# Stick-breaking attention by sigmoids and a running product, in a two-layer attention trunk

## Reference

```python
z = einsum('bhqd,bhkd->bhqk', qb, k) * scale
mask = kpos[None, :] < qpos[:, None]
log1m = where(mask, log_sigmoid(-z), 0.0)
between = cumsum(log1m, axis=3, reverse=True) - log1m
a = where(mask, exp(log_sigmoid(z) + between), 0.0)
out = einsum('bhqk,bhkd->bhqd', a, v)
```

## Time and profile before

| | us |
|---|---|
| median of 3 runs | 827.91 (827.84 to 828.54) |
| the profiled execution | 828.2 |
| its span in the profile | 826.4 |
| TensorE busy | 821.6 (99%) |
| VectorE busy | 559.7 (68%) |
| ScalarE busy | 477.8 (58%) |
| GpSimd busy | 293.7 (36%) |

### The profile page before, as it was taken

The page is one execution under the profiler, slowest core; times in us unless marked ns, Lnnn a source line. Parts: engine busy times, 40 slices in busy tenths (PEclk is TensorE's granted clock), DMA queues, the critical chain, the costliest instruction groups (busy, mean ns, idle before and its releaser), DMA issues.

```text
span 826.4 us, 11044 instructions
## 1 busy us (share of the span) xinstructions
PE 821.6 (99%) x4050; PEld 673.7 (82%) x4050; DVE 559.7 (68%) x821; ACT 477.8 (58%) x715; POOL 293.7 (36%) x297
## 2 busy tenths in 40 slices
PE   9999999999999999999999999999999999999998
PEld 5888888888888888888888888888788888888886
DVE  5576889868865666655454688898697666666542
ACT  6886655785465554543457775567844645454441
POOL 0078784404303432320000889653061044323100
PEclk9999999999999999999999999999999999999999
DMA  9745877684558777785565556878745687877652
GB/s 332 271 138 178 222 230 219 182 247 131 203 178 229 199 230 212 223 221 183 167 203 195 162 192 192 224 222 210 223 153 178 206 214 218 230 223 212 215 184 71
DMA packets 119637, 167.76 MB, mean 203 GB/s; under 512 B 56608, under 2 KB 59040, under 8 KB 119328
## 3 DMA queue, kind: packets, MB, share of 16 engines
q1 hardware_dynamic: 119296, 166.79, 66.9%
q10 hardware_dynamic: 288, 0.27, 0.1%
HBM read 153.40 MB, written 1.05 MB: 187 GB/s over the span
## 4 chain that ended last, share of the span: by engine, by line
PE 98%; DMA 1%; issue 0%; SPq 0%; ACT 0%; DVE 0%
PE acc L732 91%; PE att L812 1%; PE att L895 1%; PE att L779 1%; PE att L886 1%; DMA w_raw<-in_w_in 1%; PE att L804 1%; PE acc L812 1%; PE att L853 0%; PE att L869 0%; PE att L908 0%; PE att L972 0%; PE att L963 0%; PE att L854 0%; PE att L839 0%
## 5 line engine op out<-in xcount | busy, mean ns | idle before, releaser
L1234 DVE TENSOR_TENSOR w_lo<-w_raw,w_hi 128x1024 fp32r<-128x1024 f32 (+1 forms) x276 | 365.4, 1337 | 147.1 <-ACT w_hi L996 144.6
L732 PE MATMUL acc<-w_hi,xt 128*128 128x512 f32 (+1 forms) x1728 | 432.3, 392 | 0.5 <-ACT xt L1019 0.3
L996 ACT ACTIVATE w_hi<-w_raw 128x1024 fp32r<-128x1024 f32 (+1 forms) x275 | 286.1, 1051 | 168.7 <-PE acc L732 159.1
L732 PEld LDWEIGHTS acc<-w_hi,xt 128*128 128x128 f32 x1728 | 319.0, 188 | 66.3 <-issue 1.3
L732 PE MATMUL acc<-w_lo,xt 128*128 128x512 f32 (+1 forms) x864 | 229.9, 388 | 0.0
L732 PEld LDWEIGHTS acc<-w_lo,xt 128*128 128x128 f32 x864 | 162.0, 188 | 32.9
L1485 POOL TENSOR_SCALAR small<-small 128x2 f32<-128x2 f32 (+4 forms) x14 | 10.4, 745 | 209.2 <-ACT sq_dump L1096 132.4
L1617 POOL COPY hid_t<-hid_halves_t 128x512 uint16<-128x512 uint16 x44 | 37.7, 885 | 94.3 <-DMA hid_halves_t<-hid_halves 80.0
L1608 POOL COPY hid_halves<-hid 128x512 uint16<-128x512 uint16 x44 | 45.6, 1064 | 65.2 <-DVE hid L1311 65.2
L1625 POOL TENSOR_TENSOR merged<-merged,prod 128x1024 f32<-128x1024 f32 x10 | 32.5, 3250 | 61.2 <-DVE prod L1283 60.3
L732 PE MATMUL acc<-w_hi,ht_hi 128*128 128x512 f32 x176 | 47.7, 390 | 0.0
(11 more groups left out here) (175 smaller groups left out, 723.5 us busy)
## 6 DMA issues: line engine op xcount, KB each, us to landing
w_raw<-in_w_ffn SPq DMA_DIRECT2D x88, 512.0 KB, 4.2
w_raw<-in_w_gate SPq DMA_DIRECT2D x64, 512.0 KB, 3.9
w_raw<-in_w_ffn_down SPq DMA_DIRECT2D x44, 512.0 KB, 4.0
w_raw<-in_w_in SPq DMA_DIRECT2D x39, 512.0 KB, 4.7
w_raw<-in_w_branch SPq DMA_DIRECT2D x16, 512.0 KB, 4.1
w_raw<-in_w_out SPq DMA_DIRECT2D x16, 512.0 KB, 3.3
bg<-in_b_gate SPq DMA_DIRECT2D x8, 512.0 KB, 5.4
w_raw<-in_w_in SPq DMA_DIRECT2D x8, 396.0 KB, 3.4
```

What stands on the lines that cost most here:

```text
L732: return pe.matmul(acc[bank0 + t][:, 0:N], x_part[:, k0 + k, t * P:(t + 1) * P], w_part[:, k, 0:N], start=first, stop=last)
L996: act.activation(w_hi[:, n % WR, :, 0:N], w_raw[:, n % RAW, :, 0:N], copy).then_inc(s_hi, 1)
L1234: dve.tensor_tensor(w_lo[:, n % WR, :, 0:N], w_raw[:, n % RAW, :, 0:N], w_hi[:, n % WR, :, 0:N].bitcast(F32), ALU.subtract).then_inc(s_lo, 1)
```

## The change

Mixer A takes the form of C and D, with queries on the partitions. The scores of both pairs are computed at slot 9, the second in an idle bank of acc; the mask product goes. VectorE adds the strict mask (a constant) while it reads the banks into eb. ScalarE writes sigmoid(-z) of all four heads to a new buffer za (4 x 384 columns) and sigmoid(z) back to eb (step ssig, slot 10). VectorE runs, from the last key backwards, a scan over each head's 384 columns of za, state = max(state * za, restart), where restart is 1 at the two places where a row of queries ends (step sscan, slots 11 and 12), and multiplies eb by za shifted by one column (step smul, slots 12 and 13). GpSimd deals the halves of both pairs at slot 13 (rank 0.2, so before prep B in its queue), SyncE transposes at slots 21 and 22, ScalarE joins them into za at slots 18 and 19, and P times V reads za. The softplus, the cumulation and their constants go.

For prep B, the root moves from GpSimd to ScalarE: exp(-0.5 * ln(sum / 32 + eps)), step brs at slot 14 behind that slot's split; GpSimd waits for it. The step lambda moves from slot 14 to 15. A's maps are now the first two of eight that take turns in the transposing buffers, with buffers of their own. The constants grow from 960 to 1216 columns, and the load of the masks goes. kcs gets 128 rows, cleared at the start, and its transpose (L954) becomes a product with the identity.

```diff
-TURNS = [("C", 0), ("C", 1), ("D", 0), ("D", 1), ("D", 2), ("D", 3)]
-TURN_P = (43, 47, 52, 53, 55, 56)
+TURNS = [("A", 0), ("A", 1), ("C", 0), ("C", 1), ("D", 0), ("D", 1), ("D", 2), ("D", 3)]
+TURN_P = (21, 22, 43, 47, 52, 53, 55, 56)
...
-    "stats": 1, "stats_f": 3, "lambda": 14, "x": (0, 0, 1, 2), "f": (-2, -1, 2, 3), "m": (-1, -1, 2, 3),
+    "stats": 1, "stats_f": 3, "lambda": 15, "x": (0, 0, 1, 2), "f": (-2, -1, 2, 3), "m": (-1, -1, 2, 3),
...
-    "Ak": 7, "Az": (9, 14), "Asp": (9, 14), "Acum": (13, 17), "Apv": (21, 21), "Bq": 19, "Bk": 20,
+    "Ak": 7, "Asm": (9, 9), "ssig": 10, "sscan": (11, 12), "smul": (12, 13),
+    "Apdeal": (13, 13), "brs": 14, "Apjoin": (18, 19), "Apv": (21, 21), "Bq": 19, "Bk": 20,
...
-    "Bp": 5.5,
+    "Bp": 5.5, "smul": 2, "Apdeal": 0.2,
...
-                if kind == "z":
-                    for b in (S0, S1):
-                        pe.matmul(att[:, b, :].rearrange("p (s c) -> p s c", c=P)[:, 0:3:2, :], ident16,
-                                  mask_a.unsqueeze(1).to_broadcast([P, 2, P]), start=True, stop=False, skip_group_check=True)
...
-            def cumulate(l, step):
-
-                pe.wait_ge(dve_misc.sem, dve_misc.at(l, ("sp", step[1])))
-                for h in range(2):
-                    for i in range(2):
-                        b, part = S0 + h, sp_parts[:, h, i, :]
-                        pe.matmul(att[:, b, 0:384], tri_r[:, 0, :], part, start=False, stop=False, skip_group_check=True)
-                        mm = pe.matmul(att[:, b, P:2 * P], tri_r[:, 1, :], part[:, 256:384], start=False, stop=i == 1,
-                                       skip_group_check=True)
...
-                                           ptb[:, 2 * (m % 2) + i, 2 * s * P:(2 + s) * P],
+                                           (za if mixer == "A" else ptb)[:, 2 * (m % 2) + i, 2 * s * P:(2 + s) * P],
...
+                elif kind == "ssig":
+                    act.wait_ge(read_dve.sem, read_dve.at(l, ("sm", ("A", 1))))
+                    act.activation(za[:, :, :], eb[:, :, :], ACT.Sigmoid, scale=-1.0).then_inc(s_zc, 1)
+                    act.wait_ge(s_zc, l + 1)
+                    act.activation(eb[:, :, :], eb[:, :, :], ACT.Sigmoid).then_inc(act_misc.now(step), 1)
+                elif kind == "brs":
+                    act.wait_ge(dve_misc.sem, dve_misc.at(l, ("prep", "B")))
+                    n = NT * 2 * MIX // DD
...
+                    act.activation(rs[:, 0:n], ss[:, 0:n], ACT.Ln, scale=1.0 / DD, bias=epsb[:, 0:1]).then_inc(s_brs, 1)
+                    act.wait_ge(s_brs, l + 1)
+                    act.activation(rs[:, 0:n], rs[:, 0:n], ACT.Exp, scale=-0.5).then_inc(act_misc.now(step), 1)
...
+                elif kind == "sm" and a[0] == "A":
+                    dve.wait_ge(att_done.sem, att_done.at(l, step))
...
+                    e_free(dve, l, step)
+                    for i in range(2):
+                        e, bank = e_of(step)[0][i], score_bank(l, step, i)
+                        dve.tensor_tensor(eb[:, e, 0:P], bank[:, 0:P], strict_add[:, 1, :], ALU.add)
+                        ins = dve.tensor_tensor(eb[:, e, P:384].rearrange("p (b k) -> p b k", k=P),
+                                                bank[:, P:384].rearrange("p (b k) -> p b k", k=P), strict_add, ALU.add)
+                    ins.then_inc(read_dve.now(step), 1)
+                elif kind == "sscan":
+                    dve.wait_ge(s_zc, l + 1)
+                    for h in (2 * a, 2 * a + 1):
+                        ins = dve.tensor_tensor_scan(out=za[:, h, ::-1], data0=za[:, h, ::-1], data1=restart[:, ::-1],
+                                                     initial=0.0, op0=ALU.mult, op1=ALU.max)
+                    settled(ins)
+                elif kind == "smul":
+                    dve.wait_ge(act_misc.sem, act_misc.at(l, ("ssig", None)))
+                    h = slice(2 * a, 2 * a + 2)
+                    dve.tensor_tensor(eb[:, h, 0:383], eb[:, h, 0:383], za[:, h, 1:384], ALU.mult
+                                      ).then_inc(dve_misc.now(step), 1)
...
-                            settled(rsqrt(rs[:, 0:n], ss[:, 0:n], d, half[:, 0:n]))
+                            if a == "B":
+                                pool.wait_ge(act_misc.sem, act_misc.at(l, ("brs", None)))
+                            else:
+                                settled(rsqrt(rs[:, 0:n], ss[:, 0:n], d, half[:, 0:n]))
...
-                            pool.wait_ge(dve_misc.sem, dve_misc.at(l, ("p", a)))
+                            if a[0] == "A":
+                                pool.wait_ge(dve_misc.sem, dve_misc.at(l, ("smul", a[1])))
+                            else:
+                                pool.wait_ge(dve_misc.sem, dve_misc.at(l, ("p", a)))
```

More of the change, by code:

```diff
@@ L154, in steps @@
             put(PLAN["prep"]["BCD".index(mixer)], "prep", mixer)
-        for n in range(PAIRS[mixer] if mixer != "A" else 0):
-            put(PLAN[mixer + "sm"][n], "sm", (mixer, n))
         for n in range(PAIRS[mixer]):
-            for kind in {"A": ("z", "sp", "cum", "pv"), "B": ("p",)}.get(mixer, ("p", "pdeal", "pjoin", "pv")):
-                put(PLAN[mixer + kind][n], kind, n if mixer == "A" and kind != "pv" else (mixer, n))
+            for kind in {"A": ("sm", "pdeal", "pjoin", "pv"), "B": ("sm", "p")}.get(mixer, ("sm", "p", "pdeal", "pjoin", "pv")):
+                put(PLAN[mixer + kind][n], kind, (mixer, n))
         for m in range(MAPS[mixer]):
@@ L296 @@
 BANK_STEPS = [s for s in ORDER if banks_of(s)]
-BANK_USES = {b: [s for s in BANK_STEPS if b in banks_of(s) and s[0] != "cum"] for b in range(4)}
+BANK_USES = {b: [s for s in BANK_STEPS if b in banks_of(s)] for b in range(4)}
 def e_of(step):
     kind, a = step
-    if kind == "z":
-        return (0, 1, 2, 3), ("cum", a)
     mixer, n = a
@@ L317, in pt_slots @@
         return 2 * (a[1] % 2), 2 * (a[1] % 2) + 1
-    return (2 * a, 2 * a + 1) if kind == "cum" else (a[1],)
-PT_USES = [[s for s in ORDER if s[0] in ("cum", "pt", "pjoin") and slot in pt_slots(s)] for slot in range(4)]
+    return (a[1],)
+PT_USES = [[s for s in keys("pt", "pjoin") if s[1][0] != "A" and slot in pt_slots(s)] for slot in range(4)]
 def pv_step(s):
-    if s[0] == "cum":
-        return ("pv", ("A", s[1]))
     return ("pv", s[1])
 def trunk_kernel(nc, x, x_t, w_in, w_gate, w_branch, w_out, w_ffn, w_ffn_down,
-                 norm_g, gains, lam, cmp_pe, cmp_w, b_gate, const, masks, out):
+                 norm_g, gains, lam, cmp_pe, cmp_w, b_gate, const, out):
     with ExitStack() as ctx:
@@ L363, in trunk_kernel @@
         end_big = top[0]
+        za = place("za", [P, 4, 384], F32, at=zg_at + 4 * D_MODEL)
+        turn_at = {"p_halves": (zg_at + 16 * D_MODEL, big), "p_halves_t": (zg_at + 22 * D_MODEL, big + 4 * IN_COLS + 16)}
+        p_halves, p_halves_t = ([place(f"{name}{2 * j + i}", [P, 2, 2, 384], U16, at=at + 12 * i * MIX)
+                                 for j, at in enumerate(starts) for i in range(2)] for name, starts in turn_at.items())
         xt_raw = place("xt_raw", [P, KT, SEQ], F32, at=zg_at + 16 * D_MODEL)
@@ L412, in trunk_kernel @@
         kdup = place("kdup", [P, NT, 4, HD], F32)
-        kcs = place("kcs", [16, 2, HD], F32)
+        kcs = place("kcs", [P, 2, HD], F32)
+        epsb = place("epsb", [P, 1], F32)
         csc = place("csc", [P, NT, H, 16], F32)
@@ L534, in turned, with p_buffer @@
             return 16 * NT * (l * len(range(what % 2, N_FFN, 2)) + what // 2 + 1)
+        def p_buffer(k):
+            return k if k < 2 else 2 + k % 2
         def p_turned(l, step):
@@ L873, in times_v @@
                 mixer, m = step[1]
-                src = {"A": ("cum", m), "B": ("pt", (mixer, m))}.get(mixer, ("pjoin", (mixer, m)))
+                src = ("pt" if mixer == "B" else "pjoin", (mixer, m))
                 ev = pjoined if src[0] == "pjoin" else read_act
@@ L953, in _ @@
                             pe.wait_ge(pool_done.sem, pool_done.at(l, ("kcprep", None)))
-                            pe.transpose(att[:, TP, 0:16], kcs[:, :, :], ident[0:16, 0:16]
-                                         ).then_inc(att_done.now(step), 1)
+                            pe.matmul(att[:, TP, 0:16], kcs[:, :, :].rearrange("p m d -> p (m d)"), ident[:, 0:16],
+                                      start=True, stop=True).then_inc(att_done.now(step), 1)
                         elif kind == "cs":
```

158 lines of the change are left out of this document (60 added, 98 removed).

## The result

The changed kernel takes 829.84 us (median of 11 runs, 828.29 to 831.61), the kernel before 827.96 (11 runs, 827.58 to 828.54): a ratio of 1.0019, 95% interval 1.0010 to 1.0028. It is slower by 0.2%, where 826.9 was forecast and the range ended at 829.5. The mean granted clock of the runs goes with their time: four runs at 0.998 take 828.3 to 828.7, six at 0.995 or 0.996 take 829.6 to 830.2, one at 0.994 takes 831.6. A fall that lasts some 3.2 us at half the clock takes 0.002 off the mean (1.6 of 828), so by their clock these are runs with one, two and three of them; where the third of the last one lies no profile shows. The execution profiled is one of 829.64 us at 0.996, with a span of 827.8.

The account below looks back on a forecast made before the run. TensorE was taken to bound the kernel, busy 821.6 of 826.4 us. Of 3.3 us removed per layer 3.0 would be waited at Bq; 0.5 gained per layer gives 826.9, forecast 825.5 to 828.3, range 822.8 to 829.5.

Parts of the forecast that it names:

- rival (d): TensorE, idle 3 us at Bq, drops to 1.2 GHz afterwards, losing 1 to 2 us per layer: 829 to 831; chance 0.04.
- the sum: Whole kernel: 3.3 us of TensorE work removed per layer, 3.0 waited at Bq, 0.5 gained per layer; median 826.9.
- The products: TensorE, slot 9 and its neighbour: double scores replace mask and cumulation, 7.18 over two chunks, 3.3 us less per layer.
- The scan: VectorE, 384 columns: 0.8 us each, twice the elementwise rate, between bounds 0.40 and 2.6.
- The norm's first product: GpSimd, preparation B in layer 0: can start at 54.2 after the deals, 0.9 later than before (53.27).
- Bq: TensorE, slot 19, transposes of B's differential queries: start about 65.1 in layer 0, instead of 65.40.
- The wait: TensorE at Bq, for GpSimd's preparation of B: 3.0 of the 3.3 us removed per layer.
- The root off the path: Preparation B's root on ScalarE, done by 51.7, takes 6.7 us of GpSimd instructions off the path.
- (a): Full cut: preparation B done by 62.1, needing scans at the elementwise rate and GpSimd little disturbed; 821.3, chance 0.07.
- (b): Partial cut: scans at 0.4 to 0.6, or earlier GpSimd turns; gain 0.9 to 2.5 per layer, 823 to 826; chance 0.27.
- (c): Slower: scans above 0.9 us each put Bq after 65.40; 829.3 at 1.1 us, 841 at the upper bound; chance 0.12.
- The turns: VectorE and GpSimd alternate instructions with SBUF operands; each w_lo turn costs GpSimd 1.08 us, three remain in preparation B.

Follow-up runs that it names:

- the reordered one with the root on GpSimd: Changed kernel with both scans and products of mixer A in slot 11 ahead of w_lo, and preparation B's root back on GpSimd: 829.73 us, ratio 1.0018.
- where "o" is moved: Changed kernel with B's transposes and first scores one slot later, plus the copy of A's output moved from slot 22 to 23: 824.41 us, ratio 0.9959.

## Why the prediction was wrong

**The step that failed** is rival (d), the clock. The prediction named the mechanism and its price, "2 to 4 us at the lower level lose 1 to 2 us per layer: 829 to 831", and gave it a chance of 0.04; the sum put it at nothing. The mean clock shows at least one fall in each of the 11 runs. The price measured is 1.6 us per fall, two in most runs. The reasoning forecast a stop of 3.0 us itself and said that the trace, which has no such stop, neither shows nor excludes the fall; for the 0.04 it gave no reason. The rule of the Trainium skill ("TensorE: Matmul & The Clock Gate", "Why this matters for your kernels"), that idle gaps between bursts of products cost clock, agrees with the changed kernel's trace, and, in one of two layers, with the stop of 2.1 us put into the kernel before; stops of 1.3 to 1.6 us in three kernels' profiles did not lower it. With the sum's own stop of 3 us it deserved the largest chance; with the price measured here the forecast would have been 826.9 + 3.2, about 830. The rest of the sum was not right by luck: with the clock held up by spare products the kernel takes 826.69.

**What was right.** The products: the slot of double scores and its neighbour take 39.68 - 32.60 = 7.08 over two chunks (7.18 forecast, from the earlier trace rows). The scan: 1.80 for two, so 0.9 each (0.8 forecast), between the bounds 0.40 and 2.6; the Trainium skill's half throughput for the scan ("DVE: opcode table, instruction layouts, handler registers and perf-mode slots", "Datapath and trigger behaviour") agrees, 0.90 against 0.51 for the elementwise form of the same columns. The norm's first product: 53.47, in the time of the kernel before 54.0 (54.2 forecast). Bq: 64.93 in that time (65.1 forecast). The wait: 2.8 (3.0). The root off the path in the changed kernel: shown by its end at 50.95, 2.5 before GpSimd asks. No wait for w_lo, for the joins or in P times V.

**The rivals.** (a), the full cut, is real, but another kernel's: it needs the scans in slot 11, and not, as the rival says, at the elementwise rate, for there they take 1.81 for two. (b): its price for the scans' rate, 1.6 per layer, is what the run without the running product measures (1.57); its turns were not gained in the changed kernel. (c) did not come: undisturbed scans take 0.9 each, and Bq is still 0.47 earlier than before.

**The turns** of VectorE and GpSimd show again: four gain products take 5.79 beside three w_lo (5.14) and 2.77 without any. The difference, 3.02, is three w_lo of about 1.0. The Trainium skill ("SBUF — State Buffer", "SBUF: two separate sides") tells of a lock between the two engines, held for a whole instruction; the rows agree.

## What to carry to other kernels

Where a change removes work from the bounding engine but its feeder keeps its time, the work becomes a stop, and on TensorE a stop costs itself and then, here, for 2.8 us in most cases and for 2.1 us once in two, 1.6 us more at 1.2 GHz. Price the stop with the clock behind it, look for it in windows of 2 us (the slices of the page hide it), and before giving up on the change ask whether the feeder's chain can be ordered earlier: here two lines of the tables, one of PLAN and one of RANK, turned +0.2% into -0.9%. Two steps that shorten the same stop can each leave the kernel slower than before (829.84, 829.73), and only both together make it faster (820.95), with the clock's share on top when the stop is gone; test them together. Of a step that moves to another in-order queue, look at what stands ahead of it there.

## What was not expected of the hardware

- A stop of TensorE of 2.8 us is followed by the lower clock in most cases: both times in the profiles of the changed kernel and of the reordered one with the root on GpSimd, and by the mean clock at least once in each of the changed kernel's 11 runs. Stops of 4.6 and 5.7 us were, both times each (B a slot later; the root back on GpSimd). A stop of 2.1 us was followed by it in one layer and not in the other of the same execution. Stops of 1.3, 1.4 and 1.6 us were not, in three profiles with two each. What decides at 2.1 us is open.
- The lower level does not begin with the stop: in the changed kernel, layer 0, the clock is still 1.00 during the stop, 0.67 in the stretch in which the products start again, 0.50 in the next, and 0.98 from 68. In the longer stops it begins before they end: 0.50 from 80 to 82, with the transposes at 82.23 (B a slot later). The price is not the same for all: behind 5.7 us, Bk follows Bq by 4.63 and 4.91, against 3.22, so 1.4 and 1.7; behind 4.6 us, from the transposes to the second chunk it is 5.24 and 5.33, against 3.13 where "o" is moved, so 2.1 and 2.2.
- Spare work can pay: twelve unused products per layer make the kernel 3.15 us faster.
- GpSimd's power of 32 columns takes 5.43 us and one of 16 columns, in C's preparation, 3.52, so some 1.6 us and 0.12 a column; a scaling of 32 columns takes 0.22.
